# A wider row pitch for the hidden activations of the feed-forward stages, in a two-layer hybrid block on one core

## The chip, the cores and the metric

One core of a Trainium2 chip runs the whole program. The metric is the device time of one execution in microseconds; the median of the runs shown is used.

## What is computed

Two layers over 256 latent tokens and 256 context tokens of width 1024. Each layer is a gated feed-forward block, a token mixer (a recurrent half and a spatially gated half with one input and one output projection) and a second feed-forward block. Each has a norm, a modulation and a gate; an RMS norm ends the program. The part that the change touches is the feed-forward block:

```
def swiglu(z, w_in, w_out):
    gate, up = jnp.split(z @ w_in, 2, axis=-1)      # w_in: 1024 x 5632
    return (jax.nn.silu(gate) * up) @ w_out          # w_out: 2816 x 1024
...
h = h + 0.5 * m[2] * swiglu(modulate(rmsnorm(h, ffn1_norm_g[l]), m[0], m[1]), ffn1_w_in[l], ffn1_w_out[l])
```

Latent and context tokens share the weights. After the mixer of the second layer the context is needed no more, so the last feed-forward block works on 256 columns and all the others on 512.

## The kernel before

Activations lie with the features on the 128 partitions and the tokens (T = 512) along the row. Products keep float32 accuracy by splitting both operands into a high and a low part in the type fp32r: `w_hi` and `w_lo`, `z_hi` and `z_lo`, `h_hi` and `h_lo`. Each 128 x 128 block is then three matmuls, written out in `product` (line 437): high weights by high activations, high weights by low activations, low weights by high activations. For each the weight block is first loaded into the array (LDWEIGHTS, "PEld" in the profile), and then the activation row is streamed through it (MATMUL).

Weights come from memory in slots of 128 x 1024 floats, four in a ring: the SP queue loads a slot into `raw`, ACT rounds it to `w_hi` (L877), DVE subtracts to get `w_lo` (L1174). A block of a slot begins at a multiple of 512 bytes within the slot, and a slot is 4096 bytes per partition.

A feed-forward block is an **up stage** (44 slots; the moving operand is `z`) and a **down stage** (24 slots; the moving operand is `h`). In the up stage a pair of slots gives row jj of h: ACT takes the silu of the gate bank, DVE multiplies by the up bank (L1373), ACT writes `h_hi[:, jj, ...]` (L992) and DVE the remainder into `h_lo[:, jj, ...]` (L1378). h has KF = 22 rows of T floats, that is 2048 bytes each. In the down stage each of the 8 output tiles takes all 22 rows of h, with three matmuls for each, 66 in all. In `row` of the down stage, seven of the eight output tiles of a stage with both streams are computed on all 512 columns at once; the last tile is computed by `row_by_stream`, first on columns 0 to 255 for all k, then on columns 256 to 511. The down stage of the last block computes its eight tiles on one stream alone, on columns 112 to 367 of the rows (`LAT0 = 112`, `ALONE`); its z rows use the same columns. The latent rows that the last output projection reads, `y_hi_alone` and `y_lo_alone`, have a pitch of 1024 bytes and begin 16 floats short of a multiple of 512 bytes from `w_hi` (`y_before`).

The buffers lie in SBUF in the order of the code. By their sizes `z_hi`, `z_lo`, `w_hi` and `w_lo` each begin a multiple of 512 bytes from one another. `h_hi` begins 55,808 bytes (109 x 512) after `w_hi`, and `h_lo` another 45,056 bytes (88 x 512) after `h_hi`. With a pitch of 2048 bytes every row of h, too, begins at a multiple of 512 bytes from every block of weights.

The space of h is shared with others. While h is being filled in an up stage, its last four rows are still used by `up_acc0` and `up_acc1`, accumulators of the modulation vectors that DVE adds up in between (L1349) and TensorE sums (L452); the two unnamed buffers `up_h_hi` and `up_h_lo` put them there. In a down stage such accumulators (`down_acc`) lie in the space of `z_hi`.

PE works through its instructions in program order. `lo_ready` says that a slot is split, `slot_done` frees it, `hid_lo_ready` says that a row of h is there; `res_ready` says that a PSUM bank of the down stage has been read.

Of the kernel before, what the change touches and what calls it, by code (L numbers as in the profile page):

```python
# [6 lines left out]
F32 = mybir.dt.float32  # L7
F32R = mybir.dt.float32r
# [4 lines left out]
P = 128  # L13
D = 1024
KD = D // P
SEQ = 256
T = 512
DFF = 2816
KF = DFF // P
# [21 lines left out]
UP_MODS = {(0, 0): 4, (0, 1): 4, (1, 0): 4, (1, 1): 0}  # L41
DOWN_MODS = {(0, 0): 2, (0, 1): 1, (1, 0): 1, (1, 1): 0}
RING_FROM = 4

# [26 lines left out]
def schedule():  # L73

    at, slot, mod, ffn, tile = {}, 0, 0, 0, 0
    for l in range(DEPTH):
        for i, part in enumerate(("ffn0", "mix", "ffn1")):
# [7 lines left out]
            else:  # L85
                f = int(part[3])
                at[l, "up", f] = dict(slot=slot, mod=mod, ffn=ffn, mods=UP_MODS[l, f], first=RING_FROM)
                slot += UP_SLOTS
# [13 lines left out]
def build(nc, x_t, params, head_w, ada_w, weights, gate_w, sgu_w, sgu_b, out):  # L102
    with ExitStack() as ctx:
        def sb(name, shape, dt=F32, scope=ctx):
            return scope.enter_context(nc.sbuf_tensor(name, shape, dt))
# [44 lines left out]
            ada_head = sb("ada_head", [P, KD, KD * 2 * P], F32, head_scope)  # L150
            head_sq = sb("head_sq", [P, KD, T], F32, head_scope)
        with ExitStack() as up_scope:
            sb("up_h_hi", [P, KF - 4, T], F32, up_scope)
            up_acc = [sb("up_acc0", [P, 2, D], F32, up_scope)]
            sb("up_h_lo", [P, KF - 4, T], F32, up_scope)
            up_acc.append(sb("up_acc1", [P, 2, D], F32, up_scope))
        with ExitStack() as ffn_scope:
            h_hi = sb("h_hi", [P, KF, T], F32R, ffn_scope)
            h_lo = sb("h_lo", [P, KF, T], F32R, ffn_scope)
        with ExitStack() as y_scope:  # L160
            y_hi = sb("y_hi", [P, KD, T], F32R, y_scope)
            y_lo = sb("y_lo", [P, KD, T], F32R, y_scope)
# [1666 lines left out]
```

## Time and profile before

| | us |
|---|---|
| median of 3 runs | 1577.48 |
| lowest and highest run | 1576.68, 1584.05 |
| span of the profiled execution | 1575.5 |
| PE busy in it | 1561.2 |
| DVE, ACT, POOL busy in it | 1001.6, 631.0, 82.5 |

The span is that of one execution under the profiler, from its first to its last instruction. The page gives no other time for that execution; its span lies 2.0 us under the median. The granted clock is 1.000 in the mean, which is the 2.4 GHz level. The durations of single matmuls in the profile contain the time through the array, so they overlap; what one matmul costs in a stream of them is read as the distance between two starts.

### The profile page before, as it was taken

How to read it: one execution, taken by the hardware profiler on the slowest of the kernel's cores; microseconds unless marked ns; L12 is line 12 of the kernel's file. 1: busy time of each engine (PE TensorE's matmuls, PEld its weight loads, DVE VectorE, ACT ScalarE, POOL GpSimd, SP SyncE). 2: the span in 40 equal slices, each digit the busy share in tenths (PEclk: the TensorE clock that was granted, in tenths of full speed). 3: DMA queues.
4: the chain of work that ended last, by engine and by line, in shares of the span. 5: the costliest groups of instructions: out<-in, count | busy, mean ns of one | idle time of the engine just before them, and what ended most of it. 6: DMA issues, size and time to landing. Idle time of an engine off the chain costs nothing.

```text
span 1575.5 us, 22302 instructions
## 1 busy us (share of the span) xinstructions
PE 1561.2 (99%) x9052; PEld 1338.1 (85%) x9052; DVE 1001.6 (64%) x1243; ACT 631.0 (40%) x856; POOL 82.5 (5%) x100
## 2 busy tenths in 40 slices
PE   8999999999999999999999999999999999999998
PEld 6888888888988888888888898888888897999998
DVE  5776773783967577777364267777445358975554
ACT  4433322332784343323222243333232249764553
POOL 0000000011100200000000100000000111000001
PEclk9999999999999999999999999999999999999999
DMA  9565553653322355565353336556354323456563
GB/s 365 201 197 179 186 162 119 208 192 94 115 75 79 94 166 193 176 201 173 107 196 99 107 121 201 193 183 195 100 173 148 107 91 108 147 188 197 190 203 117
DMA packets 71786, 249.95 MB, mean 159 GB/s; under 512 B 11664, under 2 KB 11920, under 8 KB 70672
## 3 DMA queue, kind: packets, MB, share of 16 engines
q1 hardware_dynamic: 71696, 248.70, 48.1%
q8 instruction: 62, 1.02, 0.3%
q14 instruction: 28, 0.23, 0.1%
HBM read 247.62 MB, written 1.05 MB: 158 GB/s over the span
## 4 chain that ended last, share of the span: by engine, by line
PE 96%; DVE 2%; ACT 1%; issue 0%; POOL 0%; POOLq 0%; DVEq 0%; ACTq 0%
PE bank L437 85%; PE bank L574 2%; PE bank L580 2%; PE bank L576 2%; PE bank L452 1%; PE bank L475 1%; PE bank L747 1%; PE bank L720 1%; PE bank L718 1%; PE bank L719 1%; PE bank L749 0%; PE bank L468 0%; DVE w_lo L1174 0%; PE bank L529 0%; PE bank L460 0%
## 5 line engine op out<-in xcount | busy, mean ns | idle before, releaser
L877 ACT ACTIVATE w_hi<-raw 128x1024 fp32r<-128x1024 f32 x317 | 335.9, 1060 | 807.0 <-PE bank L437 792.8
L1174 DVE TENSOR_TENSOR w_lo<-raw,w_hi 128x1024 fp32r<-128x1024 f32 x317 | 387.7, 1225 | 371.9 <-ACT w_hi L877 371.6
L437 PE MATMUL bank<-z_hi,w_hi 128*128 128x512 f32 (+1 forms) x1480 | 535.9, 362 | 2.4 <-DVE w_lo L1174 1.9
L437 PE MATMUL bank<-z_lo,w_hi 128*128 128x512 f32 (+1 forms) x1480 | 532.1, 360 | 0.0
L437 PE MATMUL bank<-z_hi,w_lo 128*128 128x512 f32 (+1 forms) x1480 | 531.9, 359 | 0.0
L437 PEld LDWEIGHTS bank<-z_hi,w_hi 128*128 128x128 f32 x1480 | 278.0, 188 | 49.7 <-DVE w_lo L1174 3.2
L437 PEld LDWEIGHTS bank<-z_hi,w_lo 128*128 128x128 f32 x1480 | 278.0, 188 | 42.6
L437 PEld LDWEIGHTS bank<-z_lo,w_hi 128*128 128x128 f32 x1480 | 278.1, 188 | 42.6 <-issue 1.0
L437 PE MATMUL bank<-h_hi,w_hi 128*128 128x512 f32 (+1 forms) x770 | 266.5, 346 | 0.0
L437 PE MATMUL bank<-h_lo,w_hi 128*128 128x512 f32 (+1 forms) x770 | 265.7, 345 | 0.0
L437 PE MATMUL bank<-h_hi,w_lo 128*128 128x512 f32 (+1 forms) x770 | 265.6, 345 | 0.0
L1349 DVE SCALAR_TENSOR_TENSOR up_acc<-ada_raw,c_cols,up_acc 128x1024 f32<-128x1024 f32 x168 | 208.0, 1280 | 3.5 <-ACT up_acc L977 2.4
L437 PEld LDWEIGHTS bank<-h_hi,w_hi 128*128 128x128 f32 x770 | 145.0, 188 | 19.3 <-issue 1.2
L437 PEld LDWEIGHTS bank<-h_hi,w_lo 128*128 128x128 f32 x770 | 145.0, 188 | 18.1
L437 PEld LDWEIGHTS bank<-h_lo,w_hi 128*128 128x128 f32 x770 | 145.1, 188 | 18.0
L1373 DVE TENSOR_TENSOR scr<-scr,bank 128x512 f32<-128x512 f32 (+1 forms) x88 | 54.6, 620 | 81.9 <-PE bank L437 81.6
L1701 POOL TENSOR_TENSOR scr<-scr 128x512 f32<-128x512 f32 (+1 forms) x29 | 47.6, 1641 | 776.0 <-ACT scr L891 776.0
L1187 DVE SCALAR_TENSOR_TENSOR res<-bank,gates,res 128x256 f32<-128x256 f32 x80 | 35.7, 479 | 66.1 <-PE bank L437 66.1
L1349 DVE SCALAR_TENSOR_TENSOR down_acc<-ada_raw,c_cols,down_acc 128x1024 f32<-128x1024 f32 x56 | 75.0, 1381 | 0.6 <-ACT down_acc L977 0.4
L925 ACT ACTIVATE z_hi<-scr,n_shift 128x256 fp32r<-128x256 f32 x88 | 42.8, 506 | 50.0 <-DVE scr L1273 50.0
L574 PE MATMUL bank<-z_hi,w_hi 128*128 128x256 f32 x208 | 56.4, 286 | 0.8 <-ACT z_hi L925 0.7
L576 PE MATMUL bank<-z_hi,w_lo 128*128 128x256 f32 x208 | 55.5, 282 | 0.0
(185 smaller groups left out, 1234.3 us busy)
## 6 DMA issues: line engine op xcount, KB each, us to landing
raw<-weights SPq DMA_DIRECT2D x320, 512.0 KB, 4.1
ada_raw<-ada_w SPq DMA_DIRECT2D x128, 512.0 KB, 4.2
ada_head<-head_w SPq DMA_DIRECT2D x8, 1024.0 KB, 18.5
res<-x_t SPq DMA_DIRECT2D x4, 512.0 KB, 4.8
ada_raw<-gate_w SPq DMA_DIRECT2D x4, 256.0 KB, 5.3
ws<-sgu_w SPq DMA_DIRECT2D x2, 256.0 KB, 4.0
bs<-sgu_b SPq DMA_DIRECT2D x2, 256.0 KB, 4.2
out<-final SPq DMA_DIRECT2D x2, 256.0 KB, 3.0
```

The lines of the kernel that those rows point to most:

```text
L437: m = pe.matmul(bank[:, to], w, x[:, k, at], start=start and i == 0, stop=stop and i == 2, skip_group_check=True)
L452: m = pe.matmul(p_ada[32 * j:32 * j + 32, i * 256:i * 256 + 256], sel[:, st, :], w[:, st, :, j, :], start=(st == 0), stop=(st == 1), tile_ ...
L574: pe.matmul(banks[q][:, COLS[s]], w_hi[:, q, c], z_hi[:, k, z], start=(k == 0 and s == 0), stop=False, skip_group_check=True)
L576: pe.matmul(banks[q][:, COLS[s]], w_lo[:, q, c], z_hi[:, k, z], start=False, stop=False, skip_group_check=True)
L580: m = pe.matmul(banks[q][:, COLS[s]], w_hi[:, q, c], z_lo[:, k, z], start=False, stop=last, skip_group_check=True)
L877: act.activation(w_hi[:, r, :], raw[:, r, :], ACT.Copy).then_inc(hi_ready, 1)
L925: act.activation(z_hi[:, k, row_cols(n, s)], scr[:, k % 3, COLS[s]], ACT.Identity, bias=n_shift[:, n, k, s:s + 1]).then_inc(z_hi_ready, 1)
L1174: dve.tensor_tensor(w_lo[:, r, :], raw[:, r, :], w_hi[:, r, :].bitcast(F32), ALU.subtract).then_inc(lo_ready, 1)
L1187: m = dve.scalar_tensor_tensor(res[:, d, COLS[s]], tail_bank(d, s, n)[:, COLS[s]], gates[:, n - 1, d, s:s + 1], res[:, d, COLS[s]], ALU.mu ...
L1349: dve.scalar_tensor_tensor(acc[:, st, :], ada_raw[:, u % ADA_RING, :], c_cols[:, k, st:st + 1], acc[:, st, :], ALU.mult, ALU.add).then_inc ...
L1373: dve.tensor_tensor(scr[:, 2, 0:w], scr[:, q // 2, 0:w], pa[q][:, 0:w], ALU.mult).then_inc(hid_ready, 1)
L1701: pool.tensor_tensor(scr[:, 2, 0:w], scr[:, 2, 0:w], scr[:, d % 2, 0:w], ALU.add).then_inc(sqsum_ready, 1)
```

## The change

The rows of h get a pitch of T + 8 floats (2080 bytes) for the high parts and T + 4 floats (2064 bytes) for the low parts. Only the first T floats of a row are used. The buffers that place `up_acc0` and `up_acc1` are resized so that these still lie in the space of the last four rows of h. There are no other edits.

```
+H_HI_ROW = T + 8
+H_LO_ROW = T + 4
...
         with ExitStack() as up_scope:
-            sb("up_h_hi", [P, KF - 4, T], F32, up_scope)
+            sb("up_h_hi", [P, (KF - 4) * H_HI_ROW], F32, up_scope)
             up_acc = [sb("up_acc0", [P, 2, D], F32, up_scope)]
-            sb("up_h_lo", [P, KF - 4, T], F32, up_scope)
+            sb("up_h_lo", [P, 4 * H_HI_ROW - 2 * D + (KF - 4) * H_LO_ROW], F32, up_scope)
             up_acc.append(sb("up_acc1", [P, 2, D], F32, up_scope))
         with ExitStack() as ffn_scope:
-            h_hi = sb("h_hi", [P, KF, T], F32R, ffn_scope)
-            h_lo = sb("h_lo", [P, KF, T], F32R, ffn_scope)
+            h_hi = sb("h_hi", [P, KF, H_HI_ROW], F32R, ffn_scope)[:, :, 0:T]
+            h_lo = sb("h_lo", [P, KF, H_LO_ROW], F32R, ffn_scope)[:, :, 0:T]
```

By the sizes, row k of `h_hi` now begins 32k bytes past a multiple of 512 bytes from `w_hi`, and row k of `h_lo` 192 + 16k bytes past one, since `h_lo` itself begins 45,760 bytes after `h_hi`. On every engine the instructions and their order stay the same.

## Rows read from the trace of the kernel before

**Rows 1.** The page: busy time of each engine; the chain that ended last.

```profile
PE 1561.2 (99%) x9052; PEld 1338.1 (85%) x9052; DVE 1001.6 (64%) x1243; ACT 631.0 (40%) x856; POOL 82.5 (5%) x100
PE 96%; DVE 2%; ACT 1%; issue 0%; POOL 0%; POOLq 0%; DVEq 0%; ACTq 0%
PE bank L437 85%; PE bank L574 2%; PE bank L580 2%; PE bank L576 2%; PE bank L452 1%; PE bank L475 1%; PE bank L747 1%; PE bank L720 1%; PE bank L718 1%; PE bank L719 1%; PE bank L749 0%; PE bank L468 0%; DVE w_lo L1174 0%; PE bank L529 0%; PE bank L460 0%
```

**Rows 2.** Groups by form: line, engine, operation, tiles, shapes xcount | busy us, mean ns.

```profile
L437 PE MATMUL bank<-h_hi,w_hi 128*128 128x512 f32 x462 | 180.1, 390 | 0.0
L437 PE MATMUL bank<-h_lo,w_hi 128*128 128x512 f32 x462 | 179.8, 389 | 0.0
L437 PE MATMUL bank<-h_hi,w_lo 128*128 128x512 f32 x462 | 179.7, 389 | 0.0
L437 PE MATMUL bank<-z_hi,w_hi 128*128 128x512 f32 x1088 | 425.4, 391 | 2.4 <-DVE w_lo L1174 1.9 <-DVE z_lo L1279 0.4
L437 PE MATMUL bank<-h_hi,w_hi 128*128 128x256 f32 x308 | 86.4, 281 | 0.0
```

**Rows 3.** Timeline of PE, start us first, 81 consecutive matmuls of the first down stage.

```profile
325.78 0.39 PE L437 MATMUL bank<-h_lo,w_hi 128*128 128x512 f32 x1
...
343.91 0.39 PE L437 MATMUL bank<-h_hi,w_hi 128*128 128x512 f32 x1
```

**Rows 4.** Timeline of PE, 81 consecutive matmuls by stream, same stage, columns 0 to 255.

```profile
379.67 0.28 PE L437 MATMUL bank<-h_hi,w_hi 128*128 128x256 f32 x1
...
389.27 0.28 PE L437 MATMUL bank<-h_hi,w_lo 128*128 128x256 f32 x1
```

**Rows 5.** Timeline of PE, 90 consecutive matmuls of the last down stage, columns 112 to 367.

```profile
1519.82 0.28 PE L437 MATMUL bank<-h_lo,w_hi 128*128 128x256 f32 x1
...
1529.91 0.28 PE L437 MATMUL bank<-h_hi,w_hi 128*128 128x256 f32 x1
```

**Rows 6.** Timeline of PE in two down stages, after sums of modulations.

```profile
360.15 0.50 PE L437 MATMUL bank<-h_hi,w_hi 128*128 128x512 f32 x1
360.49 0.40 PE L437 MATMUL bank<-h_lo,w_hi 128*128 128x512 f32 x1
360.72 0.39 PE L437 MATMUL bank<-h_hi,w_lo 128*128 128x512 f32 x1
360.95 0.40 PE L437 MATMUL bank<-h_hi,w_hi 128*128 128x512 f32 x1
361.18 0.39 PE L437 MATMUL bank<-h_lo,w_hi 128*128 128x512 f32 x1
361.41 0.39 PE L437 MATMUL bank<-h_hi,w_lo 128*128 128x512 f32 x1
361.64 0.39 PE L437 MATMUL bank<-h_hi,w_hi 128*128 128x512 f32 x1
361.87 0.39 PE L437 MATMUL bank<-h_lo,w_hi 128*128 128x512 f32 x1
...
837.95 0.40 PE L437 MATMUL bank<-h_lo,w_hi 128*128 128x512 f32 x1
...
840.05 0.39 PE L437 MATMUL bank<-h_lo,w_hi 128*128 128x512 f32 x1
```

**Rows 7.** Timeline of PE, last output projection: its start, then 37 consecutive matmuls.

```profile
1358.46 0.28 PE L437 MATMUL bank<-y_hi_alone,w_hi 128*128 128x256 f32 x1
1358.58 0.28 PE L437 MATMUL bank<-y_lo_alone,w_hi 128*128 128x256 f32 x1
1358.69 0.28 PE L437 MATMUL bank<-y_hi_alone,w_lo 128*128 128x256 f32 x1
...
1363.67 0.28 PE L437 MATMUL bank<-y_hi_alone,w_lo 128*128 128x256 f32 x1
...
1367.91 0.28 PE L437 MATMUL bank<-y_hi_alone,w_lo 128*128 128x256 f32 x1
```

**Rows 8.** Windows: us, PE, PEld, DVE, ACT, POOL busy (count), clock, DMA share, GB/s.

```profile
60.00:140.00 80.00, 80.00 (x354) 66.24 (x353) 61.22 (x58) 25.66 (x33) 0.00 (x0) 1.00 0.62 204
275.00:395.00 120.00, 120.00 (x616) 101.19 (x615) 73.95 (x76) 33.58 (x37) 10.59 (x7) 1.00 0.52 164
1510.00:1560.00 50.00, 50.00 (x444) 50.00 (x443) 27.27 (x27) 26.90 (x35) 7.37 (x5) 1.00 0.57 179
```

**Rows 9.** Groups by form: the writers of h and of up_acc and down_acc.

```profile
L992 ACT ACTIVATE h_hi<-scr 128x512 fp32r<-128x512 f32 x66 | 40.5, 614 | 5.3 <-DVE scr L1373 5.3
L1378 DVE TENSOR_TENSOR h_lo<-scr,h_hi 128x512 fp32r<-128x512 f32 x66 | 45.2, 685 | 0.0
L1349 DVE SCALAR_TENSOR_TENSOR up_acc<-ada_raw,c_cols,up_acc 128x1024 f32<-128x1024 f32 x168 | 208.0, 1280 | 3.5 <-ACT up_acc L977 2.4 <-DMA ada_raw<-ada_w 1.2
L1349 DVE SCALAR_TENSOR_TENSOR down_acc<-ada_raw,c_cols,down_acc 128x1024 f32<-128x1024 f32 x56 | 75.0, 1381 | 0.6 <-ACT down_acc L977 0.4 <-DMA ada_raw<-ada_w 0.2
```

**Rows 10.** Waits: engine and line waited for, us in total, times, longest us.

```profile
DVE scr L1373 <- PE bank L437: 81.6, 80, 4.2
DVE w_lo L1174 <- ACT w_hi L877: 371.6, 260, 4.9
DVE res L1187 <- PE bank L437: 66.1, 26, 6.8
```

## The prediction

> **What bounds the kernel now.** I begin with the page [rows 1]. PE is busy for 1561.2 of 1575.5 us and makes 96% of the chain that ended last, line 437 alone 85%. Nothing else matters unless PE comes to wait for it. The granted clock is 1.00 in all the stretches read [rows 8], so its level plays no part.
>
> Next, how much of PE's work reads h. The groups by form [rows 2] give 462 matmuls of 512 columns for each of the three products, 1386 in all, and 308 of 256 columns for each, 924 in all. By the code those 924 are 3 stages x 2 streams x 66 = 396 on columns 0 to 255 or 256 to 511, and 8 x 66 = 528 in the last down stage on columns 112 to 367. The mean duration (390 ns) overlaps with the next matmul, so I don't use it as a cost; the distance between starts is the cost:
>
> - 512 columns: 80 distances in 343.91 - 325.78 = 18.13 us, **226.6 ns** each [rows 3].
> - 256 columns that begin at column 0: 80 in 389.27 - 379.67 = 9.60 us, **120.0 ns** [rows 4].
> - 256 columns that begin at column 112: 89 in 1529.91 - 1519.82 = 10.09 us, **113.4 ns** [rows 5].
>
> Rows 4 and 5 are the finding on which all rests. The work is the same, 256 columns of h through the same kind of weight block, and the distance differs by 6.6 ns. At column 0 the row of h and the block of weights begin at the same place modulo 512 bytes; at column 112 (448 bytes) they don't. So place seems to have a price. At 2.4 GHz one column takes 0.417 ns, so 256 columns need 106.7 ns and 512 need 213.3 ns. What lies on top is 13.3 ns for 512 columns, 13.3 ns for 256 at column 0 and 6.7 ns for 256 at column 112: 32, 32 and 16 columns' worth. While h streams, the weights of the next matmul are loaded (the three PEld of a k run beside PE, 101.19 of 120 us in the first down stage [rows 8]), and the two readings could get in each other's way.
>
> Two views warn that place is not all. After a pause PE doesn't find its rhythm at once: five distances take 361.64 - 360.49 = 1.15 us, 230 ns each, and in another stage nine take 2.10 us (837.95 to 840.05), 233 ns each [rows 6]. And in the last output projection, whose rows begin 64 bytes short of a multiple of 512 just as column 112 does, the distance is at first 113 to 115 ns (1358.46 to 1358.69 holds two), while later 36 of them take 4.24 us, 117.8 ns each [rows 7]. The same places thus give two distances.
>
> **The change part by part.** No instruction is added, removed or moved, and no transfer. What changes is where a row of h begins relative to the weight blocks: 32k bytes for `h_hi`, 192 + 16k bytes for `h_lo`, for k from 0 to 21, modulo 512.
>
> *The 1386 matmuls of 512 columns.* They now have the surplus of 13.3 ns at offset 0. No row shows 512 columns at another offset. The nearest rows are the two for 256 columns, and their difference is 6.6 ns. From above, the gain per matmul is bounded by the whole surplus, 13.3 ns; below nothing, rows 6 give a loss of 230 - 226.6 = 3.4 up to 233 - 226.6 = 6.4 ns. I take 6.6 ns for a pair of places that is good, and 0 for one that is not.
>
> *The 396 matmuls by stream.* Same offset, same price: 6.6 ns where the place is good, so at most 2.6 us.
>
> *The 528 of the last stage.* They are at a good place now. With the new pitch they begin at 448 + 32k and 128 + 16k bytes, modulo 512, and where such a place is bad they lose 6.6 ns each, at most 3.5 us.
>
> *The sum.* Let f be the share of good places. The gain is f x (1386 + 396) x 6.6 ns = 11.8 f us, the loss (1 - f) x 3.5 us. The only two offsets that the trace shows are one bad and one good, and the new ones are spread over the whole 512 bytes, so I take f = 1/2: 5.9 - 1.75 = **4.1 us** less, a span of 1571.4 us. With f = 1/4 the net is 0.3 us, with f = 3/4 it is 8.0 us.
>
> *The writers.* ACT writes a row of h in 614 ns and DVE in 685 ns [rows 9], 66 full rows each. Were each slower by the 8% that separates the two groups of L1349 there, that would be 66 x 0.08 x 614 ns = 3.2 us on ACT and 3.6 us on DVE over the up stages. DVE is busy for 61.22 of 80 us there and ACT for 25.66 [rows 8], and DVE waits 81.6 us for PE before L1373 [rows 10], so that covers it; without that cover PE would wait those 3 to 4 us for PSUM banks. *The accumulators.* `up_acc0` and `up_acc1` move by 576 and 992 bytes. The same operation takes 1280 ns on `up_acc` and 1381 on `down_acc` [rows 9]; if the difference were the place, 168 x 101 ns = 17 us would come onto DVE, but spread over three up stages of 44 x 24 x 0.2266 = 239 us, in which 18.8 of 80 us of DVE's time are free [rows 8], 56 us a stage. I cost both at nothing; late next would be `w_lo`, on which PE waits 1.9 us in all now [rows 2].
>
> **A rule that speaks against it.** On the trace, the start column changes the distance (rows 4 and 5), so some contention with the load is likely. The Trainium skill, "TensorE: Matmul & The Clock Gate", step-by-step part, says that TensorE has two independent read ports and that "Loading the next tile's weights doesn't steal SBUF read bandwidth from the running matmul". The trace does not agree for 256 columns, and no row tests it for 512. The same page's back-to-back gap for a lone stream is N / 2.4 + 2.5 ns, 215.8 ns at 512 columns; if good places reached it, the 1386 would give an estimated 15 us in place of 9.1.
>
> **The rivals.**
>
> - *Place plays no part at 512 columns* (17%). For it: every row of h, whatever k and slot, has 226.6 ns, and the surplus may be a fixed one for each load. Then only the short ones change: 396 x 3.3 = 1.3 us gained and 528 x 3.3 = 1.7 us lost at f = 1/2, so 1577.9 us. The rule above would give this too, without even those.
> - *Nearly every place is good* (25%). Offset 0, where both begin at the same place, may be the one bad case. With f = 0.9 the sum is 10.6 - 0.35 = 10.3 us less, 1567.2 us; with the whole surplus gone on 512 columns it would be 0.9 x (1386 x 13.3 + 396 x 6.6) ns, about 19 us less, 1558.5 us. Against it: rows 7 show a place thought good that still costs 117.8 ns.
> - *Changing places never settle* (23%), the case on the slow side. The steady 226.6 ns may be a rhythm between the stream and the load that depends on all pairs being alike. The change gives a new offset at every k, and between `h_hi` and `h_lo`. If each acts like the first matmuls after a pause [rows 6], the 1386 cost 3.4 to 6.4 ns more, 4.7 to 8.9 us, and the 528 of the last stage go to 120.0 ns, 3.5 us more: 1585.7 to 1589.9 us, in the middle 1587.8. It decides from the point where the distances of the 512-column matmuls pass 226.6 ns + (7.9 - 3.5) us / 1386 = 229.8 ns in the mean.
>
> **How the numbers follow.** The forecast (35%) is the sum with f = 1/2, set against the median of the runs, which lies 2.0 us above the profiled span: 1577.5 - 4.1 = **1573.4 us**, its own range 1569.5 to 1577.2 (f from 3/4 to 1/4). A measurement of this kernel can tell about 0.5%, 7.9 us, from no change. Of the forecast's 35% some 5 lie beyond that, so faster is 25 + 5 = 0.30; same is 30 + 17 = 0.47; slower is 0.23. The range leaves out a tenth on each side: from 1562 us (the good case halfway to its far end) to 1588 us (the middle of the slow case).
>
> **What would show it.** In the changed profile the three groups of `h` with 512 columns must be shorter, and the distance between starts in a down stage must differ with k: rows at a good offset near 220 ns, the others at 226.6 ns. If the distance is 226.6 ns for all k, the first rival holds; if their mean lies above 229.8 ns, the third. In the last down stage a mixture of 113.4 and 120.0 ns is due. The distances in the z stages (z and weights keep their places) must stay at 226.6 ns. The prediction is wrong in kind if PE starts to wait for `w_lo` or for h, since then the writers or the accumulators had a price after all.

## The result and the profile after

The changed kernel takes 1586.60 us in the median of 18 runs (1585.45 to 1591.82), the kernel before 1580.53 us in 18 runs beside them (1576.45 to 1584.86). The ratio is 1.0049, interval 1.0037 to 1.0062: the change makes the kernel **slower by 0.5%**, about 8 us. The runs of both fall into two groups, before near 1577 (9 runs) and near 1584 us (9), after near 1586 (14) and near 1591 us (4); the two profiles are of the lower groups, so they lie further apart than the medians, and e9 comes back to the groups. From lower group to lower group the loss is 9.3 us (medians 1577.1 and 1586.4). The prediction was 1573.4 us, a gain of 4.1 us; its range, 1562 to 1588 us, holds the measured time near its slow end.

The page of the changed kernel, busy time and chain, beside [rows 1]:

```profile
PE 1569.4 (99%) x9052; PEld 1340.2 (85%) x9052; DVE 1001.8 (63%) x1243; ACT 630.9 (40%) x856; POOL 82.6 (5%) x100
PE 95%; DVE 1%; ACT 1%; DMA 1%; issue 0%; SPq 0%; POOL 0%; POOLq 0%; DVEq 0%; ACTq 0%
```

The span grows from 1575.5 to 1585.2 us, 9.7 us; PE is busy for 8.2 us more. PE waits for h nowhere, and for `w_lo` 0.3 us instead of 1.9. Only its waits for the loads of `ada_head` grew, from 0.5 to 3.5 us; they belong to the start of the program, which no edit touched, and they are the DMA share of the chain. The first down stage begins 0.5 us later in all (273.0 against 272.5 us). The groups by form show where the rest comes from (line numbers are two higher than before, because of the two new constants; the fields of a line are those of [rows 2]):

```profile
L439 PE MATMUL bank<-h_hi,w_hi 128*128 128x512 f32 x462 | 182.7, 396 | 0.0
L439 PE MATMUL bank<-h_lo,w_hi 128*128 128x512 f32 x462 | 181.7, 393 | 0.0
L439 PE MATMUL bank<-h_hi,w_lo 128*128 128x512 f32 x462 | 181.9, 394 | 0.0
L439 PE MATMUL bank<-z_hi,w_hi 128*128 128x512 f32 x1088 | 425.2, 391 | 0.7 <-DVE z_lo L1281 0.4 <-DVE w_lo L1176 0.3
```

The 512-column groups on h went from 390 and 389 ns to 396, 393 and 394 ns [rows 2]; the group on z, whose rows and weights did not move, stayed at 391. ACT's and DVE's writes of h (614 and 686 ns) and the sums in `up_acc` (1279 ns) kept their durations [rows 9]. Below is the timeline of PE (starts in us) in the first and in the last down stage, 79 and 87 matmuls in a row. Each pair of lines is the first and the last of them:

```profile
326.09 0.40 PE L439 MATMUL bank<-h_lo,w_hi 128*128 128x512 f32 x1
...
344.18 0.39 PE L439 MATMUL bank<-h_lo,w_hi 128*128 128x512 f32 x1
...
1529.78 0.28 PE L439 MATMUL bank<-h_lo,w_hi 128*128 128x256 f32 x1
...
1539.97 0.28 PE L439 MATMUL bank<-h_hi,w_hi 128*128 128x256 f32 x1
```

- 512 columns on h: 18.09 us for 78 distances, 231.9 ns, against 226.6 [rows 3]. Over 1386 matmuls that is 7.3 us.
- by stream, 256 columns from column 0 or 256: 82 matmuls of the first down stage, 382.31 to 391.86 us, 9.55 us for 81 distances, 117.9 ns, against 120.0 [rows 4]. Over 396: 0.8 us less.
- last stage, 256 columns: 10.19 us for 86, 118.5 ns, against 113.4 [rows 5]. Over 528: 2.7 us.

The sum is 9.2 us of the 9.7 us by which the spans differ; the later start is the rest. The loss is all in matmuls that read h, and most of it (7.3 us) where I had expected the gain.

The sign that I had named, a distance that differs with k, is there but small: over the 7 tiles of the 3 stages the mean for a row k lies between 229.4 (k = 12) and 234.2 ns (k = 11), alike in the three stages within 1 ns, and no row comes near 220 ns.

### The profile page after: what moved, and what is told of

Same layout as the page of the kernel before. It is cut to its first block, busy times and chain, and to the rows that moved or that the text cites. A ratio compares the mean times of both kernels' runs of the same rounds, so it can differ in the third digit from the quotient of the medians.

```text
span 1585.2 us, 22302 instructions
## 1 busy us (share of the span) xinstructions
PE 1569.4 (99%) x9052; PEld 1340.2 (85%) x9052; DVE 1001.8 (63%) x1243; ACT 630.9 (40%) x856; POOL 82.6 (5%) x100
## 4 chain that ended last, share of the span: by engine, by line
PE 95%; DVE 1%; ACT 1%; DMA 1%; issue 0%; SPq 0%; POOL 0%; POOLq 0%; DVEq 0%; ACTq 0%
PE bank L439 85%; PE bank L576 2%; PE bank L582 2%; PE bank L578 2%; DMA ada_head<-head_w 1%; PE bank L454 1%; PE bank L749 1%; PE bank L722 1%; PE bank L720 1%; PE bank L721 1%; PE bank L751 0%; PE bank L531 0%; PE bank L470 0%; PE bank L462 0%; DVE w_lo L1176 0%
## 5 line engine op out<-in xcount | busy, mean ns | idle before, releaser
L1351 DVE SCALAR_TENSOR_TENSOR up_acc<-ada_raw,c_cols,up_acc 128x1024 f32<-128x1024 f32 x168 | 208.0, 1279 | 3.5 <-ACT up_acc L979 2.4
```

Of the source, the lines that this page charges most:

```text
L1351: dve.scalar_tensor_tensor(acc[:, st, :], ada_raw[:, u % ADA_RING, :], c_cols[:, k, st:st + 1], acc[:, st, :], ALU.mult, ALU.add).then_inc ...
```

## The experiments

Theory A says that a steady rhythm between stream and weight load is broken when the place changes from matmul to matmul. Theory B says that each distance between row and weights has its own price, a time from one start to the next, and that the change samples dear ones. "Distance" below is the start of the streamed row minus the start of the weight block.

### e1: the stream alone, at many places

A small kernel loads x, makes fp32r copies of it and streams 27 sections of 48 matmuls, each section on a line of its own. It leaves out the whole computation. In short form:

```
for i in range(N):          # N = 48; off and pitch differ by section
    at = off + (i % 8) * pitch
    pe.matmul(bank[j][:, 0:cols], w_hi[:, i % 8, :], room[:, at:at + cols])
```

> This kernel computes nothing of the reference: it streams 27 sections of 48 matmuls, each a fp32r block of weights against a moving row, and only the place of the row changes (512 columns: a constant offset of 0 to 480 bytes at a pitch of 2048, then pitches of 2064, 2080, 2112 and 2304 bytes; 256 columns: the same). Theory A (a pair of places that changes from matmul to matmul breaks a rhythm, a constant one does not): the 512-column sections with a constant offset all give 226.6 ns, and only the sections with pitch 2064, 2080 and 2112 give 230 ns and more; for 256 columns constant offsets give 113.4 or 120 ns. Theory B (each offset has its own price, and the change samples the dear ones): constant offsets at 512 columns differ among themselves, with several above 230 ns, and the varied pitches give about their mean. Theory C (a row that does not begin on 64 bytes is dear): offsets of 16, 32 and 480 bytes and pitches 2064 and 2080 are above 230 ns, all that are multiples of 64 bytes, pitch 2112 too, stay at 226.6 ns.

Timeline of PE in e1, one row a section (start us, then the time from first start to last end). The lines are: L64 to L69 constant offsets of 16, 32, 64, 128, 192 and 256 bytes at 512 columns, L70 to L73 of 320, 384, 448 and 480 bytes, L74 to L77 pitches of 2064, 2080, 2112 and 2304 bytes, then sections of 256 columns, L85 at 448 bytes:

```profile
28.72 11.28 PE L64 MATMUL bank<-room,w_hi 128*128 128x512 f32 x48
39.83 11.37 PE L65 MATMUL bank<-room,w_hi 128*128 128x512 f32 x48
51.04 11.15 PE L66 MATMUL bank<-room,w_hi 128*128 128x512 f32 x48
62.02 11.32 PE L67 MATMUL bank<-room,w_hi 128*128 128x512 f32 x48
73.18 11.36 PE L68 MATMUL bank<-room,w_hi 128*128 128x512 f32 x48
84.37 11.09 PE L69 MATMUL bank<-room,w_hi 128*128 128x512 f32 x48
95.30 11.17 PE L70 MATMUL bank<-room,w_hi 128*128 128x512 f32 x48
106.30 11.32 PE L71 MATMUL bank<-room,w_hi 128*128 128x512 f32 x48
117.46 11.36 PE L72 MATMUL bank<-room,w_hi 128*128 128x512 f32 x48
128.66 11.36 PE L73 MATMUL bank<-room,w_hi 128*128 128x512 f32 x48
139.85 11.24 PE L74 MATMUL bank<-room,w_hi 128*128 128x512 f32 x48
150.93 11.40 PE L75 MATMUL bank<-room,w_hi 128*128 128x512 f32 x48
162.17 11.29 PE L76 MATMUL bank<-room,w_hi 128*128 128x512 f32 x48
173.30 11.06 PE L77 MATMUL bank<-room,w_hi 128*128 128x512 f32 x48
184.20 5.92 PE L78 MATMUL bank<-room,w_hi 128*128 128x256 f32 x48
...
224.06 5.63 PE L85 MATMUL bank<-room,w_hi 128*128 128x256 f32 x48
229.52 5.84 PE L86 MATMUL bank<-room,w_hi 128*128 128x256 f32 x48
```

The distance in a section is the difference of two section starts over 48. L64 (16 bytes): (39.83 - 28.72) / 48 = 231.5 ns. L65 (32): 233.5. L66 (64): 228.8. L67 (128): 232.5. L68 (192): 233.1. L69 (256): 227.7 with its entry (the first few distances after the change of place), 226.7 once settled. L70 (320): 229.2, L71 (384): 232.5, L72 (448): 233.3. The section ahead of them, L63 at offset 0, starts at the 1.2 GHz level with distances of 427 ns; its last 24 are 226.7 ns. The varied pitches: L74 (2064) 230.8 ns, L75 (2080) 234.2, L76 (2112) 231.9, and L77 (2304, a step of 256 bytes) 227.1.

So constant offsets have prices of their own, which is theory B, and the prices repeat with 256 bytes: 256 costs what 0 does, 320 what 64 does, 384 what 128 does, 448 what 192 does, each within 0.4 ns. Theory C falls, since 64, 128 and 192 bytes differ. Most important: **at 512 columns the cheapest place is distance 0**, the one that I had taken for the bad one. At 256 columns distance 0 is dear, as rows 4 and 5 had said: L85 (448 bytes) takes (229.52 - 224.06) / 48 = 113.8 ns, with its entry, while distance 0 settles at 120.0 ns there too (L78, 184.20 to 189.95 us, 119.8 ns with its entry). But 448 bytes is the exception and not the rule: the other constant offsets of e1 and its three varied pitches lie between 116 and 120 ns.

### e5: is it the distance or the place?

The same with other offsets, and with the weights moved too (L74: both at 64 bytes, L75: both at 128, L76: row at 0 and weights at 64, L77: row at 0 and weights at 192).

> The stream of matmuls alone again, nothing of the reference computed: constant offsets that the first sweep left out, and the weights moved too. Theory B2 (the price depends on the distance between row and weights modulo 256 bytes, lowest at 0 for 512 columns): with weights and row both at 64 or both at 128 bytes 226.7 ns; weights at 64 and row at 0 the price of 192 bytes, 233.3 ns; weights at 192 and row at 0 the price of 64 bytes, 228.9 ns; all new offsets at 512 columns between 227 and 235 ns. Rival D (the row's own place counts, not the distance): both at 64 gives 228.9 ns, and weights at 64 with row at 0 gives 226.7 ns. For 256 columns around 192 bytes: 113.3 ns at 192 as at 448, and more on either side.

Timeline of PE in e5, sections L68 (96 bytes), L69 (160), L71 (224), L74 to L77, and on 256 columns L90 (row at 320 bytes, weights at 128) and L91 (row at 0, weights at 64), each with the section that follows it:

```profile
73.47 11.37 PE L68 MATMUL bank<-room,w_hi 128*128 128x512 f32 x48
84.68 11.40 PE L69 MATMUL bank<-room,w_hi 128*128 128x512 f32 x48
95.92 11.21 PE L70 MATMUL bank<-room,w_hi 128*128 128x512 f32 x48
106.96 11.36 PE L71 MATMUL bank<-room,w_hi 128*128 128x512 f32 x48
118.16 11.36 PE L72 MATMUL bank<-room,w_hi 128*128 128x512 f32 x48
...
140.60 11.05 PE L74 MATMUL bank<-room,w_hi 128*128 128x512 f32 x48
151.49 11.08 PE L75 MATMUL bank<-room,w_hi 128*128 128x512 f32 x48
162.41 11.37 PE L76 MATMUL bank<-room,w_hi 128*128 128x512 f32 x48
173.61 11.16 PE L77 MATMUL bank<-room,w_hi 128*128 128x512 f32 x48
184.61 6.21 PE L78 MATMUL bank<-room,w_hi 128*128 128x256 f32 x48
...
252.96 5.82 PE L90 MATMUL bank<-room,w_hi 128*128 128x256 f32 x48
258.61 5.62 PE L91 MATMUL bank<-room,w_hi 128*128 128x256 f32 x48
264.07 5.90 PE L92 MATMUL bank<-room,w_hi 128*128 128x256 f32 x48
```

Both at 64 bytes give (151.49 - 140.60) / 48 = 226.9 ns, both at 128 bytes 227.5 with the entry; row at 0 with weights at 64 gives 233.3 ns, the price of 192 bytes; row at 0 with weights at 192 gives 229.2, the price of 64. At 512 columns it is the distance, modulo 256 bytes, and the row's own place doesn't count (rival D falls). No distance tried at 512 columns was below that of 0. For 8 distances of the high rows, a multiple of 32 bytes each, the two sweeps give 226.7, 233.5, 228.8, 233.5 (L68 of e5, 96 bytes), 232.5, 234.2 (L69, 160 bytes), 233.1, and 233.3 (L71 of e5, 224 bytes). Their mean is 232.0 ns; the changed kernel shows 231.9. Its low rows lie at multiples of 16 bytes; of those 16 distances the sweeps hold 12, with a mean of 231.7 ns.

On 256 columns the distance does not settle the price: L90 takes (258.61 - 252.96) / 48 = 117.7 ns and L91 (264.07 - 258.61) / 48 = 113.8 ns, with their entries, and both are at a distance of 192 bytes. The dearest there is L78, 8 bytes, which settles at 126.7 ns.

### e2, e6, e7: all of h moved by a constant

The edit against the changed kernel, in e2:

```
-H_HI_ROW = T + 8
-H_LO_ROW = T + 4
+H_HI_ROW = T
+H_LO_ROW = T
...
         with ExitStack() as up_scope:
+            sb("up_pad", [P, 64], F32, up_scope)
...
         with ExitStack() as ffn_scope:
+            sb("h_pad", [P, 64], F32, ffn_scope)
```

In e6 the two pads have 16 floats (64 bytes), in e7 32 (128 bytes).

> All of h moves by 256 bytes, the pitch stays 2048 bytes. Theory A: the distance of the 512-column matmuls on h stays 226.6 ns, all k alike; the last down stage stays near 113.4 ns; time as before within 3 us. Theory B: the distance is another one, alike for all k, between 220 and 237 ns. Theory C: as A, since 256 is a multiple of 64.

e2 (88 matmuls in a row of the last up stage, on z):

```profile
1449.73 0.28 PE L441 MATMUL bank<-z_hi,w_hi 128*128 128x256 f32 x1
...
1459.97 0.28 PE L441 MATMUL bank<-z_hi,w_hi 128*128 128x256 f32 x1
```

512 columns on h, in the first down stage: 81 starts from 325.81 to 343.94 us, 18.13 / 80 = 226.6 ns, as before. Theory A had said so. Theory B had expected another distance; it fits only with the period of 256 bytes that e1 showed, and by itself this run tells nothing of the two. Yet it took 1584.9 us, against 1577.5 beside it, and nearly all of the difference is in the last two stages: 10.24 / 87 = 117.7 ns on z, whose rows did not move, and 10.12 / 86 = 117.7 ns on h (1529.82 to 1539.94 us). Their distances to the weights are, modulo 256 bytes, those of before. The expected 3 us were exceeded by something that the move does not explain; e9 comes back to it.

> All of h moves by 64 bytes at the old pitch of 2048 bytes, so every pair has one constant offset. Theory B2: 228.9 ns for each 512-column matmul on h (2.2 ns more, 3.1 us in all), 117.8 ns for the by-stream ones (0.9 us less), and 120.0 ns in the last down stage (now at 448 + 64, a multiple of 256 bytes; 3.5 us more). Theory A (only changing places cost): 226.7 ns.

e6 (80 matmuls of the first down stage; by stream, 34 in the second down stage, and 28 later in that stage, on its other 256 columns):

```profile
326.05 0.39 PE L441 MATMUL bank<-h_hi,w_hi 128*128 128x512 f32 x1
...
344.14 0.39 PE L441 MATMUL bank<-h_lo,w_hi 128*128 128x512 f32 x1
...
904.82 0.28 PE L441 MATMUL bank<-h_hi,w_hi 128*128 128x256 f32 x1
...
908.56 0.28 PE L441 MATMUL bank<-h_hi,w_hi 128*128 128x256 f32 x1
...
912.03 0.28 PE L441 MATMUL bank<-h_lo,w_hi 128*128 128x256 f32 x1
...
915.21 0.28 PE L441 MATMUL bank<-h_lo,w_hi 128*128 128x256 f32 x1
```

18.09 / 79 = 229.0 ns for 512 columns, as B says, though every pair has the same offset. Theory A, as the sole cause, falls. In the last stage 86 matmuls from 1529.79 to 1539.99 us have 10.20 / 85 = 120.0 ns, as expected. By stream 117.8 ns was expected: 58 matmuls of the first down stage, 381.51 to 388.22 us, have 6.71 / 57 = 117.7 ns, but those shown of the second have 3.74 / 33 = 113.3 ns and, after the stream has been broken off for other matmuls (L464, at 908.90 us), 3.18 / 27 = 117.8 ns. All three are at a distance of 64 bytes, so a stream of 256 columns has two rhythms at one distance and can go over from one to the other when it starts anew. The run took 1582.2 us.

> All of h moves by 128 bytes at the old pitch. Theory B2: 232.1 ns for each 512-column matmul on h (5.4 ns more, 7.5 us in all), about as much as the change itself, though no offset changes from row to row; last down stage at 64 bytes, 117.8 ns (2.3 us more). Theory A: 226.7 ns.

```profile
326.02 0.40 PE L441 MATMUL bank<-h_hi,w_hi 128*128 128x512 f32 x1
...
344.22 0.40 PE L441 MATMUL bank<-h_hi,w_hi 128*128 128x512 f32 x1
```

18.20 / 78 = 233.3 ns (79 matmuls), 6.7 ns more than at distance 0, 1.2 ns more than the expected 232.1, and more than the changed kernel's 231.9. One constant distance costs as much as the varied ones. The run took 1593.7 us; its last two stages, on z and on h, have 117.8 ns.

### e3 and e4: one half of the change at a time

The two constants have these values:

```
e3:  H_HI_ROW = T + 8, H_LO_ROW = T          e4:  H_HI_ROW = T, H_LO_ROW = T + 4
```

> Pitch 2080 bytes for the high parts alone; the low parts keep 2048 bytes and lie at a constant 192 bytes. Two of three products read the high parts. Theory A: every pair of neighbours still changes with k, so the cost is nearly the whole one: distances of about 231 ns in the mean (before 226.6, changed kernel 231.9), 7 to 9 us slower than before. Theory B and C: two thirds of the cost or so, 5 to 6 us. If only the low parts mattered it would be at 226.6 ns.

79 matmuls from 326.06 to 344.20 us: 18.14 / 78 = 232.6 ns, more than with the whole change and more than A (about 231) or B (two thirds of the cost) had said. The mean of the prices comes near it: the low rows now lie at a constant 192 bytes, 233.1 ns, and the high ones at a mean of 232.0, together 232.4. The run took 1591.1 us, 13.6 above the one beside it; its last up stage, on z, whose rows did not move, has 117.8 ns instead of 113.4, which is 1056 x 4.4 ns = 4.6 us of it.

> Pitch 2064 bytes for the low parts alone; the high parts are where they were before, the low parts begin at 16k bytes. Theory A: the third product alone changes its place from k to k, but its neighbours are disturbed by it: half of the cost or more, distances of 229 to 231 ns. Theories B and C: a third of the cost, about 228.4 ns, 2 to 4 us slower than before, and for C rows with k a multiple of 4 cost nothing.

```profile
326.14 0.40 PE L439 MATMUL bank<-h_lo,w_hi 128*128 128x512 f32 x1
...
344.19 0.40 PE L439 MATMUL bank<-h_lo,w_hi 128*128 128x512 f32 x1
```

79 matmuls: 18.05 / 78 = 231.4 ns. This is what theory A had said (229 to 231, a little exceeded) and not B: two of three matmuls have the cheap distance 0, so their prices alone would give 226.7 for two and, by the dearest section of the sweeps at a multiple of 16 bytes, at most 234.2 for one: 229.2 ns in the mean at most. The neighbour counts too. The sweep points the same way: the pitch of 2080 costs 234.2 ns, 2.2 more than the mean of its distances. In the changed kernel the same can be seen row by row. At k = 8 the high parts lie at distance 0 and the low ones at 64 bytes, which alone would cost 227.4 ns in the mean. The three matmuls of that row and the first of the next, in the changed kernel (`h_hi`, `h_lo`, `h_hi`, then k = 9):

```profile
324.46 0.39 PE L439 MATMUL bank<-h_hi,w_hi 128*128 128x512 f32 x1
...
325.15 0.39 PE L439 MATMUL bank<-h_hi,w_hi 128*128 128x512 f32 x1
```

0.69 / 3 = 230 ns, and 230.6 in the mean of all 63 distances of that row. So a cheap place can lose its gain between neighbours at other places. It is not so in every row: at k = 16 of e4, where all three lie at distance 0, the mean is 226.8 ns. What is shown is this: a constant dear distance costs up to 6.7 ns (e7, e8), and places that change can cost 2 to 3 ns more than their own prices (2.2 in the mean of e4, 3.2 at k = 8 of the changed kernel). That the mean of the prices (232.0) meets the changed kernel's 231.9 does not mean that each row pays its own price, and how the 5.3 ns divide between the two is not shown. The run took 1585.7 us.

### e8: the weights moved, the rows left

```
+        sb("w_pad", [P, 16])
         w_hi = sb("w_hi", [P, RING, SLOT], F32R)
...
+        sb("w_pad_back", [P, 48])
```

This is against the kernel before. The first pad moves the weights by 64 bytes; the second, 192 bytes behind `ada_raw`, brings what follows to a multiple of 256 bytes again.

> The kernel before with all weight slots moved by 64 bytes; rows of z, h and y keep their places, or a whole number of 256 bytes from them. Theory B2 (distance between row and weights modulo 256 bytes): every 512-column matmul, on z and y as well as on h, is now at a distance of 192 bytes and takes 233.3 ns instead of 226.7, 6.7 ns x (3264 + 1386 + 144) = 32 us; the last two stages, now at 128 bytes, near 118.7 ns, up to 8 us more; the by-stream rows gain up to 6.7 ns x 1200 = 8 us. In all 25 to 40 us slower. Rival D (the row's own place counts): 226.7 ns everywhere and the time of before.

e8, 61 matmuls of an up stage, on z:

```profile
199.82 0.39 PE L439 MATMUL bank<-z_hi,w_hi 128*128 128x512 f32 x1
...
213.82 0.39 PE L439 MATMUL bank<-z_hi,w_hi 128*128 128x512 f32 x1
```

14.00 / 60 = 233.3 ns on z and, from 326.02 to 344.22 us, 18.20 / 78 = 233.3 on h, in rows whose own places are as before up to a multiple of 256 bytes. The last two stages, now at a distance of 128 bytes, have 120.0 ns, where the bare stream had led to 118.7. The time is 1616.2 us, 38.7 above the median of the runs beside it, inside the expected 25 to 40. The rule for 512 columns holds in the whole kernel, and 64 bytes between two buffers are worth 2.5% of it.

### e9: the other distance for the last two stages

```
-LAT0 = 112
+LAT0 = 16
```

> The kernel before with the last two stages on columns 16 to 271, a distance of 64 bytes in place of 192. Both distances have shown 113.3 as well as 117.8 ns. If the two rhythms depend on how the stream enters and not on the distance, the time is as before, near 1577 or 1584 us; if 64 bytes always settles at 113.3 ns, it is near 1577 us in every run, and the median is up to 3 us better than before's; if always at 117.8, near 1584 us.

e9, 88 matmuls of the last up stage:

```profile
1449.72 0.28 PE L437 MATMUL bank<-z_hi,w_lo 128*128 128x256 f32 x1
...
1459.97 0.28 PE L437 MATMUL bank<-z_hi,w_lo 128*128 128x256 f32 x1
```

10.25 / 87 = 117.8 ns, and the 9 runs lie between 1583.7 and 1585.6 us: a ratio of 1.0033 to before (1.0018 to 1.0049). By their times, the last two stages, at a distance of 64 bytes, settled at 117.8 ns in all of them. At a distance of 192 bytes, the kernel before settled at 113.4 ns in its profile [rows 5] and e2 at 117.7 on z at the very same places. The last two stages have 1056 + 528 = 1584 matmuls on 256 columns; at 4.4 ns each that is 7.0 us, the step between before's two groups of times (1577 and 1584 us). The changed kernel's last down stage has no single distance, which leaves 1056 x 4.4 ns = 4.6 us for its groups, and they are 1586 and 1591 us. The profiles of the other runs fit: the last up stage, whose places e2, e3, e4, e6 and e7 leave alone, has 117.8 ns in e2, e3 and e7, and 113.4 in e4, e6 and the changed kernel. That this is the cause of the groups is inferred from the sizes; no profile of a 1584 us run of the kernel before was read. What makes a stream settle at the one or the other stays open; e6 and L90 and L91 of e5 show only that the distance alone does not.

No version in the study beats the kernel before. Distance 0 is the cheapest tried for 512 columns, and the one row of places that would gain, the by-stream matmuls at 64 or 192 bytes, shares its rows and weights with 512-column ones that would lose more (at 64 bytes 1386 x 2.2 ns = 3.0 us, against at most 396 x 6.7 ns = 2.7 us).

## Why the prediction was wrong

- *What bounds.* Right: PE alone; no wait for h or `w_lo` was added, and writers and accumulators cost nothing.
- *Which matmuls.* Right: 1386 + 396 + 528, and all else kept its distances.
- *"They now have the surplus of 13.3 ns at offset 0 ... I take 6.6 ns for a pair of places that is good".* This step failed. I carried the difference between two offsets at 256 columns over to 512 columns, where no row showed another offset, and took 0 for the bad place there too. It is the best: 226.7 ns, against 228.8 to 234.2 at the others read above, all that are not multiples of 256 bytes (e1, e5). The share f of places better than before at 512 columns was 0 and not 1/2, and the term of 1386 matmuls was 7.3 us of loss and not 4.6 of gain.
- *By stream.* Right in sign: 2.1 ns less, where half of 6.6 was taken; 0.8 us of gain and not 1.3.
- *Last stage.* Right in sign, a little low: 2.7 us more, where 1.75 was taken.
- *The bound.* "rows 6 give a loss of 230 - 226.6 = 3.4 up to 233 - 226.6 = 6.4 ns" held the measured 5.3 ns, and the slow rival's 1585.7 to 1589.9 us holds the measured 1586.6. That the number fits is in part luck. Its mechanism was only half right: e7 shows that a constant, dear distance costs as much as a changing one, while e4 and the row k = 8 show that neighbours at other distances do disturb each other. And the last stage, which it put at 120.0 ns, had 118.5.
- *The rule of the page.* The Trainium skill, "TensorE: Matmul & The Clock Gate", says in its step-by-step part that loading the next weights does not take read bandwidth from the running matmul. The runs speak against two reads that have nothing to do with each other: where no other engine works beside the stream, the time from start to start at 512 columns goes from 226.7 to 234.2 ns with the distance between row and weight block alone (e1, e5). That it is read bandwidth that is lost is not shown; the loads themselves last 188 ns at 256 bytes and 187 ns at 448 (L69 and L72 of e1). The same page's gap for a lone stream, an estimate of 215.8 ns by its formula, was reached at none of the places.
- *The rivals "place plays no part at 512 columns" and "nearly every place is good"* fall with the same runs.

The two steady distances of rows 7 (113 and 117.8 ns at the same places) were noted and then not used. They were a warning that a place does not have one price, so that its price need not have the same sign for streams of two lengths. My picture is that of two periodic reads, the row's and the weights', that meet in one way or another; no run shows the meeting itself.

## What to carry to other kernels

In this kernel, where TensorE is the bound and weights are loaded for every fp32r matmul, the distance between the streamed row and the weight block modulo 256 bytes is worth 3% of a 512-column matmul. In a kernel of this kind, keep it at 0 for 512 columns, check that padding or a new buffer ahead of either does not move it, and measure it for each width by itself. A price measured at one shape does not carry its sign to another. A sweep of the bare stream, 27 sections in one run of 260 us, gives the sign before the kernel is touched. Its prices came out within 1.3 ns in the kernel where all places were alike (e6, e7, e8); where they were mixed their mean was 2 ns or more too low in e4.

## What the runs showed of the hardware

- A 512-column fp32r matmul with its weight load takes 226.7 ns at distance 0 modulo 256 bytes, 13.3 ns above its 512 columns at 2.4 GHz; 228.8 ns at 64 bytes, 230.0 at 48 (L67 of e5, 62.43 to 73.47 us), 231.5 at 16, 232.5 at 128, 233 to 234 at 32, 96, 160, 192, 224, 240 and 248 (L72 and L73 of e5, 118.16 to 129.36 and to 140.60 us).
- In a stream whose distances change from matmul to matmul the cheap ones need not be cheap: 230.6 ns at k = 8 of the changed kernel, where their own prices give 227.4.
- A 256-column one takes 120.0 ns at distance 0 and 113.3 or 117.8 at 64 and at 192 bytes. An unbroken stream kept its rhythm once it had settled, and a restarted one could take the other: e6 shows 113.3 and 117.8 at 64 bytes in one stage, e9 117.8; before shows 113.4 at 192 bytes, e2 117.7.
- Moving the weights by 64 bytes made this kernel 38.7 us slower (e8), with every instruction and their order the same and only addresses changed.
